# Expert stage of a two-layer diffusion backbone: loop over token tiles unrolled, weights made slot by slot on ScalarE

## The chip, the cores and the metric

The kernel runs on 1 core of one Trainium2 chip, which has a TensorE (PE, matmul), a VectorE (DVE), a ScalarE (ACT), a GpSimd (POOL) and a SyncE (SP), and 16 DMA engines. The metric is the device time of one execution in microseconds; less is better.

## The reference, cut to what matters

Two trunk layers work on 256 context and 512 latent tokens of width 1024. Each has a mixer and then an expert layer (PEER) with 8 heads; each head picks 16 of 16384 single-neuron experts for each token. Layer 0 runs the experts for all 768 tokens, layer 1 for the 512 latent ones.

```python
def peer_ffn(xn, wq, keys1, keys2, u_tab, v_tab):
    q = (xn @ wq).reshape(t, PEER_HEADS, PEER_D_KEY)
    s1 = jnp.einsum('thd,hkd->thk', q[..., :half], keys1)
    s2 = jnp.einsum('thd,hkd->thk', q[..., half:], keys2)
    v1, i1 = lax.top_k(s1, PEER_TOPK)
    v2, i2 = lax.top_k(s2, PEER_TOPK)
    cand = (v1[..., :, None] + v2[..., None, :]).reshape(t, PEER_HEADS, PEER_TOPK * PEER_TOPK)
    cs, ci = lax.top_k(cand, PEER_TOPK)
...
    expert = e1 * PEER_N_KEYS + e2
    gate = jax.nn.softmax(cs, axis=-1)
...
        ub = u_tab[eb]
        vb = v_tab[eb]
        act = jax.nn.gelu(jnp.einsum('td,thkd->thk', xb, ub), approximate=False)
        return jnp.einsum('thk,thkd->td', gb * act, vb)
```

The result is multiplied by a gate row and added to the stream h. All is float32.

## The kernel before, in words

`backbone` runs the modulation rows, mixer 0, the expert stage of layer 0 (6 tiles of 128 tokens), mixer 1, the expert stage of layer 1 (4 tiles) and a final norm. The change lies in `peer_stage` (L1128 to L1521) and the constants ahead of it.

A tile has TS = 128 slots: 8 heads of 16 chosen experts. For each slot POOL issues one indirect DMA (L1217) that gathers for each of the 128 tokens its own expert's row, 1024 numbers of u and 1024 of v, 8 KB for each partition and 1.05 MB in all, into one of RING = 8 ring buffers. Over both layers that is 10 tiles and 1280 gathers.

What is done with a slot, in order: VectorE multiplies the u half by the normalised tokens f and sums it (the dot, L1492, with an accumulator read). ScalarE makes Gelu of two dots at once (L1285). VectorE multiplies it by 1/sum and by the exponentials of the softmax (`coefficients`, L1459), for a pair of slots (PAIR = 2), and does so behind the first dot of the next pair. ScalarE scales the identity by each of the two coefficients (the diagonal, L1288). TensorE multiplies diagonal and v half, two 512-column matmuls per slot (L1372; the trace has four instructions for them), and adds up the 16 slots of a head in one of two PSUM pairs. The last matmul's semaphore `slot_free` lets POOL gather into this ring buffer again. Per head VectorE adds the PSUM pair to y (`head_sum`, L1467 and L1469), and at a tile's end multiplies y by the gate row and adds it to h (L1517, L1519). It waits for TensorE before both, and only then copies the next tile's f (L1485).

While the slots of a tile run, the next tile is prepared: the norm (ScalarE L1225 and L1228, VectorE L1391 to L1400 into fn), transposes, queries and scores on TensorE (L1307 to L1331) with copies on ScalarE, and **routing** on VectorE (`route`, L1402): for each head four pieces, top 16 of the first scores, top 16 of the second, top 16 of their 256 sums, and the table index. Its small instructions are chained by a semaphore (`link`, L1406). One piece is put behind each pair g (2 slots), four pairs for each head:

```python
ROUTE_NOW = {3: 6, 8: 7}
ROUTE_FIRST = {4 * n: LAG + n for n in range(NH - LAG)}
ROUTE_NEXT = {33 + 4 * n: n for n in range(NH - LAG)}
```

So heads 0 to 5 of the next tile are routed in slots 66 to 113, and heads 6 and 7 in the early slots of their own tile. In the first tile of a layer, heads 0 and 1 (LAG = 2) come before its first dot, and 2 to 7 in its slots 0 to 47. ScalarE makes Exp for one head at a time (`gate`, L1272), with a table load before it and one before the next Gelu.

Order of work: each engine has its own straight program, tied to the others by semaphores. The first and the last tile of each layer are written out; the tiles between (4 in layer 0, 2 in layer 1) are one loop body (`tiles`, L1190, `eng.Fori`) on each engine, and waits in it compare with a register. Waits inside a chain are followed by a semaphore increment of their own (`wait_apart`, L1180).

## Time and profile before

| what | value |
|---|---|
| median of 3 runs | 4596.92 us (4594.8 to 4597.45) |
| the profiled execution: span from first to last instruction | 4610.2 us |
| the profiled execution's own time | only its span is given |
| PE busy | 3609.0 us, 78% |
| DVE busy | 2865.6 us, 62% |
| ACT busy | 1156.5 us, 25% |
| POOL busy | 1501.2 us, 33% |
| gathers | 1280, 1342.26 MB, 72.4% of 16 engines' span |
| TensorE's mean granted clock | 0.921 |

How to read it: the span is one execution, taken by the hardware profiler, and it lies 13.3 us above the median of the runs. Busy times of the engines overlap. A busy PE is not a PE at its peak, since matmuls are pipelined. The granted clock is the share of TensorE's full clock. The rows further on name an engine, a source line, the operation, output and inputs by the program's names, shapes, how often, busy us and mean ns, and behind the bar the idle time ahead of it with what ended it.

### The profile page before, as it was taken

To read this page: it belongs to the slowest core of one execution; us is meant where nothing else is said; L and a number is where in the kernel's file an instruction comes from. 1 tells how busy PE (TensorE), PEld (TensorE's weight loads), DVE (VectorE), ACT (ScalarE), POOL (GpSimd) and SP (SyncE) were. 2 spreads that over 40 slices of the span, in tenths; PEclk is the share of its full clock that TensorE was granted. 3 is DMA by queue.
4 is the path that set the end of the run, shared out by engine and by line. 5 is a ranking of instruction groups with operands and counts; after the bars stand their busy time and mean duration, and the time that the engine had idled before them with its cause. 6 is when DMAs were issued, how large, how long until landed. Compare 5 with 4: busy or idle time off the path is not lost. (4 is left out here: it accounts for less than half of the span.)

```text
span 4610.2 us, 39123 instructions
## 1 busy us (share of the span) xinstructions
PE 3609.0 (78%) x10024; PEld 1742.9 (38%) x10024; DVE 2865.6 (62%) x7037; ACT 1156.5 (25%) x2826; POOL 1501.2 (33%) x1338
## 2 busy tenths in 40 slices
PE   8899968778768777777777778996877876877776
PEld 1288643323323323322322226784332332332222
DVE  2222358776766776676686555664877677677655
ACT  1121113222222222222222122561322222222212
POOL 0103114444434443443444331001443444344332
PEclk9998689999989999998999998998998999899899
DMA  8612059999999998998999982004999999899998
GB/s 297 245 64 73 10 205 369 388 373 392 398 358 366 409 373 361 398 378 341 415 375 394 421 370 92 1 1 170 372 392 377 374 400 383 357 406 383 381 421 342
DMA packets 233040, 1455.55 MB, mean 316 GB/s; under 512 B 25141, under 2 KB 25141, under 8 KB 67813
## 3 DMA queue, kind: packets, MB, share of 16 engines
q0 software_dynamic: 184320, 1342.26, 72.4%
q1 hardware_dynamic: 48392, 110.79, 6.7%
q8 instruction: 62, 1.02, 0.1%
q14 instruction: 170, 1.38, 0.1%
q10 hardware_dynamic: 96, 0.10, 0.0%
HBM read 1447.72 MB, written 5.34 MB: 315 GB/s over the span
## 5 line engine op out<-in xcount | busy, mean ns | idle before, releaser
L1372 PE MATMUL peer_py<-peer_ring,peer_diag 128*128 128x512 f32 x5120 | 2506.7, 639 | 874.8 <-ACT peer_diag L1288 874.5
L1217 POOL DMA_INDIRECT peer_ring<-in_uv_dram,peer_idx x1280 | 1416.6, 1107 | 2123.8 <-PE peer_py L1372 1848.4
L1492 DVE CUSTOM_DVE_ANT_0 peer_ring<-peer_ring,peer_f 128x1024 f32<-128x1024 f32 x1280 | 1565.6, 1226 | 769.4 <-DMA peer_ring<-in_uv_dram,peer_idx 722.8
L1372 PEld LDWEIGHTS peer_py<-peer_ring,peer_diag 128*128 128x128 f32 x5120 | 996.7, 202 | 2353.2 <-issue 1194.2
L1288 ACT ACTIVATE peer_diag<-ident,peer_coef 128x128 f32<-128x128 f32 x1280 | 444.1, 394 | 1880.1 <-DVE peer_coef L1459 1880.1
L1285 ACT ACTIVATE peer_gel<-peer_u 128x2 f32<-128x2 f32 x640 | 129.9, 203 | 733.8 <-DVE peer_u L1492 732.9
L318 DVE TENSOR_TENSOR m_w_low<-m_w_low_plain,m_w_high 128x2048 fp32r<-128x2048 f32 x26 | 61.0, 2347 | 218.1 <-ACT m_w_high L313 218.0
L326 PE MATMUL m_ps<-m_w_high,m_aT_high 128*128 128x512 f32 x416 | 164.8, 396 | 3.5 <-DVE m_v L750 1.8
L1208 POOL IOTA peer_iota<- 128x16 f32 x2 | 0.3, 144 | 503.8 <-POOLq L765 363.6
L326 PE MATMUL m_ps<-m_w_low,m_aT_high 128*128 128x512 f32 x416 | 162.6, 391 | 0.0
L1459 DVE SCALAR_TENSOR_TENSOR peer_coef<-peer_gel,peer_grec,peer_gexp 128x2 f32<-128x2 f32 x640 | 138.3, 216 | 10.0 <-ACT peer_gel L1285 9.9
L326 PE MATMUL m_ps<-m_w_high,m_aT_low 128*128 128x512 f32 x368 | 143.9, 391 | 0.0
L176 PE MATMUL mod_ps<-arena,silu 128*2 128x512 f32 x256 | 113.7, 603 | 17.9 <-DMA arena<-in_ada_w_dram 17.9
L1314 PE MATMUL peer_pb<-arena,peer_fT 128*128 128x512 f32 x256 | 120.3, 592 | 0.0
L1469 DVE TENSOR_TENSOR peer_y<-peer_y,peer_py 128x1024 f32<-128x1024 f32 x70 | 85.1, 1216 | 48.7 <-PE peer_py L1372 48.7
L1285 ACT ACT_TABLE_LOAD x84 | 107.8, 1283 | 1.5
L1492 DVE DVE_READ_ACCUMULATOR2_ANT peer_u<- 128x1 f32 x1280 | 104.7, 82 | 0.0
L313 ACT ACTIVATE m_w_high<-m_w_low_plain 128x2048 fp32r<-128x2048 f32 x26 | 49.8, 1913 | 209.5 <-DMA m_w_low_plain<-in_ev_w_in_dram 101.8
L1272 ACT ACT_TABLE_LOAD x78 | 100.1, 1283 | 1.4
L992 PE MATMUL m_ps<-m_aT_high_plain,m_aT_low_plain 128*128 128x128 f32 x576 | 84.2, 293 | 6.2 <-ACT m_aT_high_plain L889 5.8
L326 PEld LDWEIGHTS m_ps<-m_w_high,m_aT_high 128*128 128x128 f32 x416 | 78.7, 189 | 20.2 <-DVE m_v L750 2.0
L992 PEld LDWEIGHTS m_ps<-m_aT_high_plain,m_aT_low_plain 128*128 128x128 f32 x576 | 71.7, 197 | 35.0 <-ACT m_aT_low_plain L874 24.9
(198 smaller groups left out, 2915.7 us busy)
## 6 DMA issues: line engine op xcount, KB each, us to landing
arena<-in_ada_w_dram SPq DMA_DIRECT2D x16, 2048.0 KB, 8.9
peer_ring<-in_uv_dram,peer_idx POOLq DMA_INDIRECT x1280, 9.3
mod_rows_sb<-in_ada_w_dram SPq DMA_DIRECT2D x8, 2048.0 KB, 9.1
m_w_low_plain<-in_ev_w_in_dram SPq DMA_DIRECT2D x12, 1024.0 KB, 5.0
arena<-in_peer_wq_dram SPq DMA_DIRECT2D x2, 4096.0 KB, 18.4
mod_rows_sb<-mod_rows SPq DMA_DIRECT2D x7, 1024.0 KB, 7.0
m_w_low_plain<-in_od_w_in_dram SPq DMA_DIRECT2D x6, 1024.0 KB, 5.2
m_w_low_plain<-in_ev_w_out_dram SPq DMA_DIRECT2D x4, 1024.0 KB, 5.0
```

The lines of the kernel that those rows point to most:

```text
L176: ins = pe.matmul(ps[:, n % 4], silu[:, :, k], ada[n % ring][:, k], start=k == 0, stop=k == KC - 1)
L326: ins = pe.matmul(out, l, r, start=j % 2 == 0 and kl == 0 and m == 0, stop=j % 2 == 1 and kl == KH - 1 and m == 2)
L992: ins = pe.matmul(PS[:, 4 + m // 4, (m % 4) * P:(m % 4 + 1) * P], pr[:, i % 3, m * P:(m + 1) * P], dg[:, i % 2], start=True, stop=True, sk ...
L1217: pool.indirect_dma_start(ring[:, s % RING], None, A["uv"], bass.IndirectOffsetOnAxis(idx[:, hd, j:j + 1], 0)).then_inc(sem(f"landed{s % R ...
L1272: act.activation(gexp[:, hd], cs[:, hd], ACT.Exp, bias=negm[:, hd:hd + 1], accum_out=gsum[:, hd:hd + 1]).then_inc(sem("gexp"), 1)
L1285: act.activation(gel[:, g % 4], u[:, g % 4], ACT.Gelu).then_inc(sem("gelu"), 1)
L1288: act.activation(diag[:, (PAIR * g + j) % RING], ident[:], ACT.Copy, scale=coef[:, g % 4, j:j + 1]).then_inc(sem("diag"), 1)
L1314: ins = pe.matmul(PB[:, 2 + b], fT[:, k], wq[:, k, b * HALF:(b + 1) * HALF], start=k == 0, stop=k == KC - 1)
L1372: ins = pe.matmul(PY[:, hd % 2, b], diag[:, s % RING], ring[:, s % RING, D + b * HALF:D + (b + 1) * HALF], start=s % TOPK == 0, stop=s % T ...
L1459: dve.scalar_tensor_tensor(coef[:, g % 4], gel[:, g % 4], grec[:, hd:hd + 1], gexp[:, hd, at:at + PAIR], ALU.mult, ALU.mult).then_inc(sem( ...
L1469: dve.tensor_tensor(y[:], y[:], ps, ALU.add).then_inc(sem("y_free"), 1)
L1492: dve.tensor_tensor_reduce(x, x, f[:], 1.0, 0.0, ALU.mult, ALU.add, u[:, g % 4, j:j + 1]).then_inc(sem("dot"), 1)
```

## The change

- The tile loop is gone: every engine's program is written out for all tiles, and all waits compare with constants. POOL's waits and the links lose the extra semaphore increment.
- Slot by slot (`weight`): ScalarE makes Gelu of one slot, multiplies it by the normalised gate (a Copy with a scale per partition) and makes the diagonal, each with a wait on its own step before. VectorE's `coefficients` is gone.
- `combine`: all 128 slots of a tile are summed in one PSUM pair, which alternates from tile to tile. `head_sum` is gone; `add_up` multiplies the PSUM pair by the gate row and adds it to h, behind dot 4 of the next tile.
- f, cs, idx and the gates are double-buffered; fn and its copy are gone.
- The softmax: VectorE subtracts the top score for a batch of heads, ScalarE makes one Exp for the batch, and VectorE sums, inverts and multiplies (`normalise`). Batches are 4 heads; in a layer's first tile 2, 3 and 3.
- Routing: in the first tile of a layer the own heads 2 to 7 as before, one piece every second slot in slots 0 to 47. The next tile's 32 pieces are spread evenly from slot 45 (first tile: 52) to slot 120.
- Queries, their transposes and scores are made in two halves.

```diff
@@
+TS = NH * TOPK
+PIECES = 4
+ACT_SQUARE, DVE_MEAN, ACT_ROOT, DVE_MOD = 1, 3, 5, 8
+PE_F_T, ACT_F_T, PE_Q = 11, 14, 16
+ACT_Q, PE_Q_T, ACT_Q_T, PE_S, ACT_S = (25, 33), (27, 35), (29, 37), (31, 39), (34, 42)
+FIRST_GATES, GATES = ((0, 2), (2, 5), (5, 8)), ((0, 4), (4, 8))
+def own_piece(s):
+    return (LAG + s // 2 // PIECES, s // 2 % PIECES) if s % 2 == 0 and 0 <= s // 2 < (NH - LAG) * PIECES else None
+def next_piece(s, start, n=NH * PIECES):
+    span = TS - 5 - start
+    for m in range(n):
+        if start + m * span // n == s:
+            return divmod(m, PIECES)
+    return None
@@ POOL
+            for i in range(first, last + 1):
+                for s in range(TS):
+                    n, (hd, k) = i * TS + s, divmod(s, TOPK)
+                    if k == 0:
+                        pool.wait_ge(sem("idx"), i * NH + hd + 1)
+                    if n >= RING:
+                        pool.wait_ge(sem("slot_free"), n - RING + 1)
+                    pool.indirect_dma_start(ring[:, n % RING], None, A["uv"], bass.IndirectOffsetOnAxis(idx[:, i % 2, hd, k:k + 1], 0)
+                                            ).then_inc(sem(f"landed{n % RING}"), 16)
@@ ScalarE
-                    act.wait_ge(sem("dot"), i * TS + PAIR * (g + 1))
-                    act.activation(gel[:, g % 4], u[:, g % 4], ACT.Gelu).then_inc(sem("gelu"), 1)
-                    act.wait_ge(sem("coef"), i * PAIRS_T + g + 1)
-                    for j in range(PAIR):
-                        act.activation(diag[:, (PAIR * g + j) % RING], ident[:], ACT.Copy, scale=coef[:, g % 4, j:j + 1]
-                                       ).then_inc(sem("diag"), 1)
+            def exponents(i, b):
+                lo, hi = gates_of(i)[b]
+                act.wait_ge(sem("shifted"), batch_ready(i, lo))
+                act.activation(gexp[:, lo:hi], shifted[:, lo:hi], ACT.Exp).then_inc(sem("gexp"), 1)
+            def weight(i, s):
+                n, (hd, k) = i * TS + s, divmod(s, TOPK)
+                at = slice(n % RING, n % RING + 1)
+                act.wait_ge(sem("dot"), n + 1)
+                act.activation(gel[:, at], u[:, at], ACT.Gelu).then_inc(sem("gelu"), 1)
+                if k == 0:
+                    act.wait_ge(sem("gate"), batch_ready(i, hd))
+                act.wait_ge(sem("gelu"), n + 1)
+                act.activation(coef[:, at], gel[:, at], ACT.Copy, scale=gate[:, i % 2, hd, k:k + 1]).then_inc(sem("coef"), 1)
+                act.wait_ge(sem("coef"), n + 1)
+                act.activation(diag[:, n % RING], ident[:], ACT.Copy, scale=coef[:, at]).then_inc(sem("diag"), 1)
@@ TensorE
+            def combine(i, s):
+                n = i * TS + s
+                if s == 0 and i >= 2:
+                    pe.wait_ge(sem("y"), i - 1)
+                pe.wait_ge(sem("diag"), n + 1)
+                for b in range(2):
+                    ins = pe.matmul(PY[:, i % 2, b], diag[:, n % RING], ring[:, n % RING, D + b * HALF:D + (b + 1) * HALF],
+                                    start=s == 0, stop=s == TS - 1)
+                ins.then_inc(sem("slot_free"), 1)
@@ VectorE
-                dve.scalar_tensor_tensor(coef[:, g % 4], gel[:, g % 4], grec[:, hd:hd + 1], gexp[:, hd, at:at + PAIR],
-                                         ALU.mult, ALU.mult).then_inc(sem("coef"), 1)
+            def below_top(i, b):
+                lo, hi = gates_of(i)[b]
+                c = cs[:, i % 2, lo:hi]
+                dve.tensor_tensor(shifted[:, lo:hi], c, c[:, :, 0:1].broadcast_to([P, hi - lo, TOPK]), ALU.subtract
+                                  ).then_inc(sem("shifted"), 1)
+            def normalise(i, b):
+                lo, hi = gates_of(i)[b]
+                dve.wait_ge(sem("gexp"), batch_ready(i, lo))
+                link(dve.tensor_reduce(gsum[:, lo:hi], gexp[:, lo:hi], AX.X, ALU.add))
+                link(dve.reciprocal(grec[:, lo:hi], gsum[:, lo:hi]))
+                dve.tensor_tensor(gate[:, i % 2, lo:hi], gexp[:, lo:hi],
+                                  grec[:, lo:hi].rearrange("p (h o) -> p h o", o=1).broadcast_to([P, hi - lo, TOPK]), ALU.mult
+                                  ).then_inc(sem("gate"), 1)
+            def add_up(i):
+                dve.wait_ge(sem("slot_free"), (i + 1) * TS)
+                if i == first:
+                    dve.wait_ge(S("peer_gates"), 16 * rows_loads)
+                dve.tensor_tensor(y[:], PY[:, i % 2].rearrange("p b n -> p (b n)"), rows[:, kind(i - shift), 2], ALU.mult).then_inc(sem("y"), 1)
+                dve.wait_ge(sem("y"), i + 1)
+                link(dve.tensor_tensor(h[:, i - shift], h[:, i - shift], y[:], ALU.add))
...
+            dve.wait_ge(sem("idx"), first * NH + LAG)
+            below_top(first, 0)
+            normalise(first, 0)
+            for i in range(first, last + 1):
+                for s in range(TS):
+                    dot(i, s)
+                    if i > first and s == 4:
+                        add_up(i - 1)
+                    if i < last:
+                        if s == DVE_MEAN:
+                            mean(i + 1)
+                        if s == DVE_MOD:
+                            modulate(i + 1)
+                    for tile, piece, past in ((i, own_at(i, s), own_at(i, s - 3)), (i + 1, next_at(i, s), next_at(i, s - 3))):
+                        if piece is not None:
+                            route(tile, *piece)
+                        if batch_ending(tile, piece) is not None:
+                            below_top(tile, batch_ending(tile, piece))
+                        if batch_ending(tile, past) is not None:
+                            normalise(tile, batch_ending(tile, past))
+            add_up(last)
```

## Rows read from the trace of the kernel before

**Rows 1.** Page, part 2: mean busy share of the DMA engines, 40 slices of the span

```profile
DMA  8612059999999998998999982004999999899998
```

**Rows 2.** Table by stretch: length, busy us per engine, clock, DMA share, GB/s

```profile
1225.00:1330.00 105.00, 78.78 (x153) 30.62 (x154) 90.97 (x263) 30.18 (x75) 47.06 (x38) 0.92 0.97 377
...
1465.00:1565.00 100.00, 86.41 (x223) 36.87 (x221) 58.55 (x125) 20.63 (x61) 41.56 (x41) 0.98 1.01 420
```

**Rows 3.** Waits, 1225 to 1330 us: sum, times, longest in us

```profile
DVE peer_ring L1492 <- DVE peer_topi L1418: 1.5, 8, 0.2
```

**Rows 4.** Waits, 1465 to 1565 us

```profile
DVE peer_ring L1492 <- DMA peer_ring<-in_uv_dram,peer_idx: 38.9, 32, 2.3
```

**Rows 5.** From issue of a gather to landing, 1225 to 1330, then 1465 to 1565 us

```profile
DMA to landing us min/median/max: 6.4/8.2/10.6
...
DMA to landing us min/median/max: 7.5/9.9/11.0
```

**Rows 6.** Timeline, end of layer 0: two dots ten slots apart, one group of matmuls

```profile
2706.17 1.23 DVE L1492 CUSTOM_DVE_ANT_0 peer_ring<-peer_ring,peer_f 128x1024 f32<-128x1024 f32 x1 [1.11 <-DMA peer_ring<-in_uv_dram,peer_idx]
...
2710.51 3.70 PE L1372 MATMUL peer_py<-peer_ring,peer_diag 128*128 128x512 f32 x8 [1.27 <-ACT peer_diag L1288]
...
2731.00 1.23 DVE L1492 CUSTOM_DVE_ANT_0 peer_ring<-peer_ring,peer_f 128x1024 f32<-128x1024 f32 x1 [1.11 <-DMA peer_ring<-in_uv_dram,peer_idx]
```

**Rows 7.** Timeline of VectorE while routing: start us, us, engine, line, operation

```profile
1302.71 1.23 DVE L1492 CUSTOM_DVE_ANT_0 peer_ring<-peer_ring,peer_f 128x1024 f32<-128x1024 f32 x1
...
1304.00 1.22 DVE L1492 CUSTOM_DVE_ANT_0 peer_ring<-peer_ring,peer_f 128x1024 f32<-128x1024 f32 x1
...
1307.33 1.29 DVE L1492 CUSTOM_DVE_ANT_0 peer_ring<-peer_ring,peer_f 128x1024 f32<-128x1024 f32 x1 [0.19 <-DVE peer_topi L1418]
...
1312.01 1.29 DVE L1492 CUSTOM_DVE_ANT_0 peer_ring<-peer_ring,peer_f 128x1024 f32<-128x1024 f32 x1 [0.19 <-DVE peer_topi L1418]
...
1318.17 1.23 DVE L1492 CUSTOM_DVE_ANT_0 peer_ring<-peer_ring,peer_f 128x1024 f32<-128x1024 f32 x1
...
1324.38 1.23 DVE L1492 CUSTOM_DVE_ANT_0 peer_ring<-peer_ring,peer_f 128x1024 f32<-128x1024 f32 x1
```

**Rows 8.** Page, part 5: head sums

```profile
L1469 DVE TENSOR_TENSOR peer_y<-peer_y,peer_py 128x1024 f32<-128x1024 f32 x70 | 85.1, 1216 | 48.7 <-PE peer_py L1372 48.7
```

**Rows 9.** Timeline of VectorE at a seam between tiles (1345 to 1432 us)

```profile
1372.32 0.69 DVE L1485 COPY peer_f<-peer_fn 128x1024 f32<-128x1024 f32 x1 [5.62 <-issue]
1377.61 1.23 DVE L1492 CUSTOM_DVE_ANT_0 peer_ring<-peer_ring,peer_f 128x1024 f32<-128x1024 f32 x1 [4.59 <-issue]
...
1378.76 1.22 DVE L1492 CUSTOM_DVE_ANT_0 peer_ring<-peer_ring,peer_f 128x1024 f32<-128x1024 f32 x1
```

**Rows 10.** First and last dot of all, last dot of layer 0, first of layer 1

```profile
L1492 DVE CUSTOM_DVE_ANT_0 peer_ring<-peer_ring,peer_f x1280: 1204/1225/1297, 661.5 to 4585.1; 128x1024 f32<-128x1024 f32 x183
...
2750.88 1.23 DVE L1492 CUSTOM_DVE_ANT_0 peer_ring<-peer_ring,peer_f 128x1024 f32<-128x1024 f32 x1 [1.06 <-DMA peer_ring<-in_uv_dram,peer_idx]
...
3206.58 1.23 DVE L1492 CUSTOM_DVE_ANT_0 peer_ring<-peer_ring,peer_f 128x1024 f32<-128x1024 f32 x1
```

**Rows 11.** Page, part 5, and Exp in the groups of 1200 to 1550 us

```profile
L1288 ACT ACTIVATE peer_diag<-ident,peer_coef 128x128 f32<-128x128 f32 x1280 | 444.1, 394 | 1880.1 <-DVE peer_coef L1459 1880.1
L1285 ACT ACTIVATE peer_gel<-peer_u 128x2 f32<-128x2 f32 x640 | 129.9, 203 | 733.8 <-DVE peer_u L1492 732.9
...
L1285 ACT ACT_TABLE_LOAD x84 | 107.8, 1283 | 1.5
...
L1272 ACT ACTIVATE peer_gexp<-peer_cs,peer_negm 128x16 f32<-128x16 f32 x8 | 2.5, 308 | 0.1
```

**Rows 12.** Timeline of the first tile: dots of slots 16 and 32

```profile
708.44 1.23 DVE L1492 CUSTOM_DVE_ANT_0 peer_ring<-peer_ring,peer_f 128x1024 f32<-128x1024 f32 x1
...
752.99 1.23 DVE L1492 CUSTOM_DVE_ANT_0 peer_ring<-peer_ring,peer_f 128x1024 f32<-128x1024 f32 x1
```

**Rows 13.** Timeline of TensorE after a longer pause

```profile
1320.02 5.38 PE L1372 MATMUL peer_py<-peer_ring,peer_diag 128*128 128x512 f32 x8 [2.39 <-ACT peer_diag L1288]
```

More of the change, by code:

```diff
@@ L1363, in body @@
-            def body(i, now, nxt):
-                for g in range(PAIRS_T):
-                    hd = g // PAIRS
-                    if g % PAIRS == 0:
-                        pe.wait_ge(sem("y_free"), i * NH + hd + 1)
-                    for j in range(PAIR):
-                        s = PAIR * g + j
-                        pe.wait_ge(sem("diag"), i * TS + s + 1)
-                        for b in range(2):
-                            ins = pe.matmul(PY[:, hd % 2, b], diag[:, s % RING], ring[:, s % RING, D + b * HALF:D + (b + 1) * HALF],
-                                            start=s % TOPK == 0, stop=s % TOPK == TOPK - 1)
-                        ins.then_inc(sem("slot_free"), 1)
-                    if not nxt:
+                    queries(first, part, k)
@@ L1376, in body @@
+                q_transposes(first, part)
+                scores(first, part)
+            for i in range(first, last + 1):
+                for s in range(TS):
+                    combine(i, s)
+                    if i == last:
                         continue
-                    if g == PE_F_T:
+                    if s == PE_F_T:
                         f_transposes(i + 1)
-                    if PE_Q <= g < PE_Q + KC:
-                        queries(i + 1, g - PE_Q)
-                    if g == PE_Q_T:
-                        q_transposes(i + 1)
@@ L1383, in body @@
-                    if PE_S <= g < PE_S + 2:
-                        scores(i + 1, g - PE_S)
-            tiles(pe, body)
+                    if PE_Q <= s < PE_Q + 2 * KC:
+                        queries(i + 1, (s - PE_Q) // KC, (s - PE_Q) % KC)
+                    for part in range(2):
+                        if s == PE_Q_T[part]:
+                            q_transposes(i + 1, part)
+                        if s == PE_S[part]:
+                            scores(i + 1, part)
         @block.vector
@@ L1402, in route @@
[L1402 to L1423 removed]
+                link(dve.reciprocal(ss[:, 3:4], ss[:, 2:3]))
@@ L1424, in route @@
+            def route(i, hd, piece):
+                if piece == 0 and hd % 4 == 0:
+                    dve.wait_ge(sem("s"), 2 * i + hd // 4 + 1)
                 if piece < 2:
@@ L1521, in _ @@
-            tiles(dve, body)
+            dve.wait_ge(sem("idx"), first * NH + LAG)
+            below_top(first, 0)
+            normalise(first, 0)
+            for i in range(first, last + 1):
+                for s in range(TS):
+                    dot(i, s)
+                    if i > first and s == 4:
+                        add_up(i - 1)
+                    if i < last:
+                        if s == DVE_MEAN:
[9 more added lines that the diff above has]
+                            normalise(tile, batch_ending(tile, past))
```

332 lines of the change are left out of this document (110 added, 222 removed).

## The prediction

> **What bounds the kernel now.** I first read the page's slices by time [rows 1]: outside the first fifth and the short mixer stage in the middle, the 16 DMA engines are busy in nine tenths of nearly every slice, so the two expert stages look bound by the gathers. The table by stretch [rows 2] shows that this is two cases. From 1465 to 1565 us the gathers move 420 GB/s and VectorE is busy for 58.55 of 100 us. From 1225 to 1330 us, where VectorE also routes the next tile, they move 377 GB/s at a share of 0.97, and VectorE is busy for 90.97 of 105 us. The waits settle who leads. In the routing stretch VectorE's dot product never waited for a landing: the longest wait before it is 1.5 us in sum, for its own routing [rows 3]. In the other it waited 32 times, 38.9 us, for a landing [rows 4]. The time from issue to landing agrees: median 8.2 us while routing, 9.9 us else [rows 5], so at 2.7 and 2.5 us per slot some 3.0 and 4.0 gathers are in flight. A busy share near 1 is no sign of a full queue here: fewer are in flight, and each packet is open longer.
>
> So there are two paces. **DMA's pace:** ten slots of the last tile of layer 0 take 2731.00 - 2706.17 = 24.83 us, 2.483 us per slot [rows 6]. **Routing pace:** four pairs with the four pieces of one head take 1324.38 - 1302.71 = 21.67 us, 2.71 us per slot [rows 7], and a head sum of 1.22 us [rows 8] comes on top every 16 slots. A third loss is the seam between tiles: VectorE drains TensorE (48.7 us of waiting before head sums, 10 times [rows 8]) and then stands 5.62 and 4.59 us at "issue" around a loop's end [rows 9]. From the first to the last dot, layer 0 takes 2750.88 - 661.5 = 2089.4 us for 767 intervals and layer 1 4585.1 - 3206.58 = 1378.5 us for 511 [rows 10]: 3467.9 us, 2.713 per slot. At DMA's pace these 1278 intervals would take 3173 us; some 295 us are the most that the expert stages can give.
>
> **The change part by part.**
>
> VectorE, per pair of slots: two dots and a coefficient take 1304.00 - 1302.71 = 1.29 plus 1.15, 2.44 us; back to back dots without one are 1378.76 - 1377.61 = 1.15 us apart [rows 7, 9], so 2.30 us stay. The pieces cost 4.62, 4.68, 6.16 and 6.21 less 2.44 each: 2.18, 2.24, 3.72 and 3.77, 11.9 us per head. They stay, less two one-column instructions (a negation, a reciprocal), which I put at 0.1 us each. Per tile the change adds one subtraction, one sum, one reciprocal and one product for each batch of heads, some 1 us per batch of small instructions (estimate from the 0.1 to 0.3 us steps inside the pieces); it comes twice per tile and is in the jitter below.
>
> Spread over 78 slots, one head's pieces fall on 9.75 slots: 11.9 + 9.75 x 1.15 = 23.1 us, 2.37 us per slot, under 2.483. VectorE stops being the bound there, but is filled to 95%. In the first tile of each layer the own heads 2 to 7 still fall on 8 slots each: (11.7 + 9.2) / 8 = 2.62 us for 48 slots; its next-tile pieces fall on 8.9 slots, (11.9 + 10.2) / 8.9 = 2.49, level with DMA.
>
> ScalarE: per slot a Gelu (0.203), a coefficient and a diagonal (0.394) [rows 11]. The coefficient has no row: at least the Gelu's 0.203, at most the 0.308 of an Exp of 16 columns with a per-partition operand [rows 11]; I take 0.3. With two waits on itself, 0.05 to 0.3 us each (the trace has none of this kind), a slot takes 1.0 to 1.5 us of 2.483: it hides behind the gathers. Were that cover gone, ScalarE would set 1.5 us, still below the dot's pace with pieces. Exp in batches leaves 22 in place of 80, so most table loads of 1.28 us [rows 11] go; they were hidden, and I count nothing. A late batch would hold the next Gelu for about 3 us, and behind it diagonal, matmul, slot and gather; the ring covers that.
>
> The ring: before, a pair's coefficient is made only after the next pair's first dot, so the first slot of a pair waits from 1302.71 to past 1307.33 + 1.2 = 1308.5 [rows 7] before its diagonal is begun. After, the diagonal is ready 1.0 to 1.5 us behind the dot. Slots come free about 5 us earlier, two gathers more in flight. That is what lets the DMA queue stay full over a piece of 3.7 us.
>
> TensorE: the same matmuls into one PSUM pair, 3.70 us per two slots [rows 6], 1.85 of 2.483. The seven other head sums per tile vanish and the tile's last is folded into the gate product, off the seam: VectorE does it behind dot 4 of the next tile while eight slots are in the ring. The seam's drain and the loop's end go. What would be late next there is nothing but the landing of the next slot.
>
> POOL issues the same 1280 gathers; waits on constants replace register waits; it is queued behind nothing new. idx and cs are doubled, so the next tile's indices, spread to slot 120, are there before POOL wants them. SP has the same loads.
>
> **The sum.** Layer 0: 48 x 2.62 + 719 x 2.483 = 125.8 + 1785.3 = 1911.1; layer 1: 125.8 + 463 x 2.483 = 1275.4. Together 3186.5, a gain of 281.4 us. Less:
> - routing stretches at 2.533 rather than 2.483. The bounds are 2.483 and 2.71 [rows 6, 7]; I take a value near the lower, because VectorE no longer leads by its rows, and add 0.05 for jitter: 78 slots x 8 tiles x 0.05 = 31 us;
> - mean and modulation of the next tile, 3 us of VectorE in the part of each first tile where it leads: 6 us;
> - before the first dot, the first Exp batch now ends behind both heads' routing and VectorE waits for it: 1.28 + 0.31 us [rows 11] and three small steps, 2.5 us per layer: 5 us;
> - back: at each stage's end one head sum (1.22) and one slot's matmuls (1.85) are no longer in the tail: 6 us.
>
> 281.4 - 31 - 6 - 5 + 6 = 245 us. Against the profiled span of 4610.2 us that is 4365; that execution lies 13.3 us above the median of the runs, 4596.9, and the same saving there gives **4352 us**.
>
> The Trainium skill, "DMA: Bandwidth & Descriptors", Anatomy of one DMA, fits bytes / 436e3 us behind a fixed part; for 1.05 MB that is 2.405 us per slot, an estimate that would put the sum near 4352 - 1230 x 0.078 = 4256 us. The trace does not agree: 2.483 us is held over ten slots.
>
> **The rivals.**
>
> Gathers are the bound in routing stretches as well. For it: their share is 0.97 there, and 377 / 0.97 = 389 GB/s would be 2.70 us per slot whatever VectorE does [rows 2]. Against it: no dot waits for a landing [rows 3]. Then 624 slots take 2.70: 135 us in place of 31, 4456 us. A ring that runs dry behind each long piece ends between the two. Chance 0.20.
>
> Straight code starves an engine's instruction fetch, which the loop bodies did not. For it: the 5.62 and 4.59 us at "issue" [rows 9] show what a missing fetch costs. Against it: the first tile is straight code already, and its second head takes 752.99 - 708.44 = 44.55 us [rows 12], as 2 x 21.67 + 1.22 = 44.6 in a loop body. With one such pair of stalls per tile, 10 x 10.2 = 102 us: 4454 us. Chance 0.08.
>
> On the other side: **TensorE's clock.** Eight matmuls that follow 2.39 us of idle time took 5.38 rather than 3.70 us [rows 13]: part of them ran at the lower of the two levels, 1.2 in place of 2.4 GHz. Now TensorE gets one slot at a time, with a pause after each, and behind a piece of 3.7 us it stands for about 3 us. At the lower level throughout a slot takes some 3.5 us, more than 2.483, and TensorE leads: each such slot adds 1.0 us that the ring cannot give back. From 245 / 1.02 = 240 such slots on, 38% of the 624, the change is slower than before; if all 624 are, 4352 - 31 + 624 x 1.02 = 4957 us. Against it: in the DMA-bound stretch, with pauses of 1.27 us between pairs [rows 6], the granted clock is 0.98 [rows 2], and per-slot pauses are shorter (2.483 - 1.85 = 0.63). A backlog also fills the pause behind a piece. Chance 0.06, of which 0.05 slower.
>
> The Trainium skill, "TensorE: Matmul & The Clock Gate", HAM oscillation, describes this rival: a kernel whose matmul groups are short beside the waits between them is throttled again at each wait. By that rule the routing stretches would fall to it; the trace agrees only in so far as a pause of over 2 us was followed by slow matmuls.
>
> **How the numbers follow.** The forecast has 0.66, with its own range of 4310 to 4400 (no jitter at all; half of the way to 2.70). The two rivals near 4455 have 0.28, the clock 0.06. The range of 4305 to 4460 leaves out the clock rival and some of what lies beyond the others. About 0.2% is what a measurement of this kernel can tell from no change: faster 0.94, same 0.01, slower 0.05.
>
> **What the new profile would show.** Right: dots 2.48 to 2.55 us apart over whole tiles, also in slots 45 to 123; DMA near 415 GB/s in every full slice; dots that wait for landings in the routing stretches; no gap at the seam beyond a slot's; median issue to landing over 11 us; ScalarE busy about 1 us per slot. The forecast is wrong if the routing stretches keep 2.7 us per slot with waits for landings (first rival), if "issue" ends many waits (second), or if the granted clock falls under 0.8 and gathers wait for TensorE (third).

## The result and the profile after

The changed kernel takes 4339.51 us (median of 4 runs, 4336.71 to 4348.3) against 4597.18 us before (median of 4, 4594.8 to 4603.24): a ratio of 0.9437, 95% interval 0.9423 to 0.945. That is 257.7 us less, where 245 were forecast. The profiled execution has a span of 4334.8 us and a time of its own of 4336.71 us.

From the page of the changed kernel: the slices by time (PEclk is the granted TensorE clock in tenths), the groups of the expert stages, and the issue of the gathers with its median time to landing.

```profile
span 4334.8 us, 33292 instructions
PEclk9899599999999999999999999998999999999999
DMA  8712029999999999999999982003999999999998
L1445 DVE CUSTOM_DVE_ANT_0 peer_ring<-peer_ring,peer_f 128x1024 f32<-128x1024 f32 x1280 | 1556.1, 1224 | 918.6 <-DMA peer_ring<-in_uv_dram,peer_idx 909.9
L1228 POOL DMA_INDIRECT peer_ring<-in_uv_dram,peer_idx x1280 | 1451.7, 1134 | 1817.9 <-PE peer_py L1345 1692.5
L1275 ACT ACTIVATE peer_diag<-ident,peer_coef 128x128 f32<-128x128 f32 x1280 | 513.8, 401 | 41.7
L1273 ACT ACTIVATE peer_coef<-peer_gel,peer_gate 128x1 f32<-128x1 f32 x1280 | 377.1, 295 | 46.7 <-ACT peer_gel L1269 0.4
peer_ring<-in_uv_dram,peer_idx POOLq DMA_INDIRECT x1280, 14.9
```

The DMA slices look much as in [rows 1], only with fewer 8s, so the busy share again says little. What has changed is who waits. The dots wait for landings for 909.9 us in sum, and that nearly everywhere but in the first 48 slots of each layer. The next two fences are the second tile, which routes the third: the table by stretch (length, busy us of PE, PEld, DVE, ACT, POOL, clock, DMA share, GB/s), for that tile and for the last tile of layer 0, which routes nothing; then the waits of the second tile (sum, times, longest).

```profile
980.00:1300.00 320.00, 262.26 (x588) 102.81 (x587) 228.14 (x540) 127.66 (x399) 147.58 (x128) 0.97 1.01 420
2270.00:2580.00 310.00, 245.72 (x496) 84.09 (x496) 155.27 (x250) 111.40 (x373) 120.20 (x120) 1.00 1.00 416
```

```profile
POOL peer_ring L1228 <- PE peer_py L1345: 166.1, 118, 4.1
DVE peer_ring L1445 <- DMA peer_ring<-in_uv_dram,peer_idx: 86.5, 79, 2.1
```

Where the routing stretch moved 377 GB/s before [rows 2], a whole routing tile now moves 420, as much as the one without routing (its stretch from 1145 to 1265 us, about slots 68 to 116, moves 419). Of its 128 dots 79 wait for a landing, where before no such wait was seen [rows 3]. VectorE no longer leads.

The seam between the first and the second tile, timeline: the last two dots of the old tile, the first of the new.

```profile
970.03 1.22 DVE L1445 CUSTOM_DVE_ANT_0 peer_ring<-peer_ring,peer_f 128x1024 f32<-128x1024 f32 x1 [1.25 <-DMA peer_ring<-in_uv_dram,peer_idx]
...
972.51 1.23 DVE L1445 CUSTOM_DVE_ANT_0 peer_ring<-peer_ring,peer_f 128x1024 f32<-128x1024 f32 x1 [1.25 <-DMA peer_ring<-in_uv_dram,peer_idx]
...
975.00 1.23 DVE L1445 CUSTOM_DVE_ANT_0 peer_ring<-peer_ring,peer_f 128x1024 f32<-128x1024 f32 x1 [1.25 <-DMA peer_ring<-in_uv_dram,peer_idx]
```

It is a slot like any other, 2.49 us, where the drain and the loop's end [rows 9] made gaps of 11.4 to 21.8 us. Worked out from the starts of the dots in both traces, us per 16 slots (at 2.483 per slot: 39.7):

```
slots           0-15  -31   -47   -63   -79   -95   -111  -127+seam   tile
before, tile 0  47.0  44.5  44.3  38.1  46.7  44.5  44.3  49.3       358.7
before, tile 1  40.0  42.7  41.5  39.8  45.0  44.5  44.5  59.4       357.5
after,  tile 0  39.8  37.8  40.1  43.3  40.9  40.1  41.5  38.1       321.5
after,  tile 1  40.7  39.7  40.1  40.6  41.9  38.1  41.2  40.2       322.7
after,  tile 6  39.8  37.7  39.8  45.0  39.4  40.3  41.4  38.9       322.1
```

From the first to the last dot, layer 0 now takes 2582.7 - 653.5 = 1929.2 us and layer 1 4313.3 - 3028.3 = 1285.0 us: 3214.2 us, or 2.515 per slot for 1278 intervals, against 3467.9 before [rows 10]. The other 21.7 us of the spans' difference (275.4) lie outside: the first dot comes 8.0 us earlier, the way from the last dot of layer 0 to the first of layer 1 is 10.1 us shorter (445.6 for 455.7), and the tail 3.6.

Part of the early start is one thing that the diff does and the prediction never priced. Routing of head 0 ahead of the first dot, VectorE's timeline. Before (first instruction, one link inside, first of the next head):

```profile
637.11 0.29 DVE L1414 MAX8 peer_top<-peer_scores 128x8 f32<-128x128 f32 x1 [16.99 <-ACT peer_scores L1266]
...
638.31 0.29 DVE L1417 MAX8 peer_top<-peer_scores 128x8 f32<-128x128 f32 x1
...
638.75 0.09 DVE L1418 MATCH_VALUE_LOAD peer_topi<-peer_top,peer_scores 128x8 f32 x1
...
648.86 0.29 DVE L1414 MAX8 peer_top<-peer_scores 128x8 f32<-128x128 f32 x1 [0.17 <-DVE peer_idx L1445]
```

After:

```profile
633.62 0.29 DVE L1396 MAX8 peer_top<-peer_scores 128x8 f32<-128x128 f32 x1 [17.11 <-ACT peer_scores L1257]
...
634.66 0.29 DVE L1399 MAX8 peer_top<-peer_scores 128x8 f32<-128x128 f32 x1
...
634.99 0.09 DVE L1400 MATCH_VALUE_LOAD peer_topi<-peer_top,peer_scores 128x8 f32 x1
...
642.98 0.28 DVE L1396 MAX8 peer_top<-peer_scores 128x8 f32<-128x128 f32 x1
```

The durations are the same, the steps between are not: from one instruction to the one that needs its result it took 0.44 us, now 0.33; one head took 11.75 us and takes 9.36. In the kernel before every such wait is followed by a semaphore increment on VectorE; the change leaves it out. Experiment 3 gives that 2.07 us of a head's 2.39.

The other surprise is in the first tile of each layer. Timeline of the first tile, slots 46 to 51:

```profile
769.45 0.17 DVE L1424 TENSOR_SCALAR peer_idx<-peer_ef 128x16 uint32<-128x16 f32 x1
...
769.72 1.02 ACT L1257 ACTIVATE peer_scores<-peer_pb 128x1024 f32<-128x1024 f32 x1 [12.23 <-DVE peer_idx L1424]
...
771.65 7.75 PE L1345 MATMUL peer_py<-peer_ring,peer_diag 128*128 128x512 f32 x14 [11.25 <-ACT peer_diag L1275]
...
775.38 0.94 POOL L1228 DMA_INDIRECT peer_ring<-in_uv_dram,peer_idx  x1 [13.13 <-PE peer_py L1345]
```

ScalarE's second copy of the next tile's scores, put behind slot 42, overwrites scores that own head 7 is still routed from; that ends at slot 46. So ScalarE stands 12.23 us with the weights of several slots queued behind the copy, TensorE and then POOL stand with it (POOL issues nothing for 13.13 us), and the dots of slots 51 and 52 wait 2.43 and 2.18 us for their landings, twice the usual 1.25. These are the 43.3 and 45.0 in the table.

### The profile page after: what moved, and what is told of

Same layout as the page of the kernel before. It is cut to its first block and busy times, and to the rows that moved or that the text cites. A ratio compares the mean times of both kernels' runs of the same rounds, so it can differ in the third digit from the quotient of the medians.

```text
span 4334.8 us, 33292 instructions
## 1 busy us (share of the span) xinstructions
PE 3589.7 (83%) x10024; PEld 1674.6 (39%) x10024; DVE 2684.7 (62%) x6235; ACT 1564.1 (36%) x4522; POOL 1536.3 (35%) x1338
## 5 line engine op out<-in xcount | busy, mean ns | idle before, releaser
L1445 DVE CUSTOM_DVE_ANT_0 peer_ring<-peer_ring,peer_f 128x1024 f32<-128x1024 f32 x1280 | 1556.1, 1224 | 918.6 <-DMA peer_ring<-in_uv_dram,peer_idx 909.9
L1228 POOL DMA_INDIRECT peer_ring<-in_uv_dram,peer_idx x1280 | 1451.7, 1134 | 1817.9 <-PE peer_py L1345 1692.5
L1345 PEld LDWEIGHTS peer_py<-peer_ring,peer_diag 128*128 128x128 f32 x5120 | 929.3, 194 | 2148.7 <-ACT peer_diag L1275 1320.4
L1269 ACT ACTIVATE peer_gel<-peer_u 128x1 f32<-128x1 f32 x1280 | 258.8, 202 | 1827.0 <-DVE peer_u L1445 1825.7
L1275 ACT ACTIVATE peer_diag<-ident,peer_coef 128x128 f32<-128x128 f32 x1280 | 513.8, 401 | 41.7
L1273 ACT ACTIVATE peer_coef<-peer_gel,peer_gate 128x1 f32<-128x1 f32 x1280 | 377.1, 295 | 46.7 <-ACT peer_gel L1269 0.4
L1320 PE MATMUL peer_pb<-arena,peer_fT 128*128 128x512 f32 x320 | 164.6, 612 | 2.4 <-ACT peer_fT L1242 2.4
L1320 PEld LDWEIGHTS peer_pb<-arena,peer_fT 128*128 128x128 f32 x320 | 62.5, 197 | 81.3 <-issue 81.1
L990 PE MATMUL m_ps<-m_aT_high_plain,m_aT_low_plain 128*128 128x128 f32 x576 | 84.5, 294 | 7.2 <-ACT m_aT_high_plain L887 5.8
L254 POOL TENSOR_TENSOR m_a<-m_a,mod_rows_sb 128x1024 f32<-128x1024 f32 x6 | 15.1, 2518 | 202.9 <-DVE m_a L238 202.9
L324 PEld LDWEIGHTS m_ps<-m_w_low,m_aT_high 128*128 128x128 f32 x416 | 78.9, 190 | 16.8
## 6 DMA issues: line engine op xcount, KB each, us to landing
peer_ring<-in_uv_dram,peer_idx POOLq DMA_INDIRECT x1280, 14.9
```

Of the source, the lines that this page charges most:

```text
L324: ins = pe.matmul(out, l, r, start=j % 2 == 0 and kl == 0 and m == 0, stop=j % 2 == 1 and kl == KH - 1 and m == 2)
L990: ins = pe.matmul(PS[:, 4 + m // 4, (m % 4) * P:(m % 4 + 1) * P], pr[:, i % 3, m * P:(m + 1) * P], dg[:, i % 2], start=True, stop=True, sk ...
L1228: pool.indirect_dma_start(ring[:, n % RING], None, A["uv"], bass.IndirectOffsetOnAxis(idx[:, i % 2, hd, k:k + 1], 0)).then_inc(sem(f"lande ...
L1269: act.activation(gel[:, at], u[:, at], ACT.Gelu).then_inc(sem("gelu"), 1)
L1273: act.activation(coef[:, at], gel[:, at], ACT.Copy, scale=gate[:, i % 2, hd, k:k + 1]).then_inc(sem("coef"), 1)
L1275: act.activation(diag[:, n % RING], ident[:], ACT.Copy, scale=coef[:, at]).then_inc(sem("diag"), 1)
```

## The experiments

Questions: how the gain divides between the loop's end, the increments, the spread of the routing, the early weights and the seam; and what the 41 us are that the stages still lie above 1278 x 2.483 = 3173. Two kernels start from the old one, the others from the new.

**1. Old kernel, loop written out.**

```diff
-            body(first, ROUTE_FIRST, ROUTE_NEXT)
-            with eng.Fori(first + 1, first + n_tiles - 1) as i:
-                body(i, ROUTE_NOW, ROUTE_NEXT)
-            body(first + n_tiles - 1, ROUTE_NOW, {})
+            last = first + n_tiles - 1
+            for i in range(first, last + 1):
+                body(i, ROUTE_FIRST if i == first else ROUTE_NOW, ROUTE_NEXT if i < last else {})
```

> The kernel before with its tile loop written out, nothing else. Theory (a loop's end costs at the seam): the four seams behind a loop's end are some 10.5 us longer per tile in the trace of before (355 to 357 us against 345 to 347 us), so 4597 - 42 = 4555 us. Rival (the loop's end is hidden by the ring, the long seams have another cause): 4597 us.

Measured 4553.86 us (before on the same chip 4603.97), 0.9893 [0.9877, 0.991]: 50 us, where 42 were expected. The seam of tile 0 in its timeline:

```profile
1000.66 1.23 DVE L1491 CUSTOM_DVE_ANT_0 peer_ring<-peer_ring,peer_f 128x1024 f32<-128x1024 f32 x1 [1.11 <-DMA peer_ring<-in_uv_dram,peer_idx]
...
1007.28 1.22 DVE L1468 TENSOR_TENSOR peer_y<-peer_y,peer_py 128x1024 f32<-128x1024 f32 x1 [4.90 <-PE peer_py L1371]
...
1011.78 1.23 DVE L1491 CUSTOM_DVE_ANT_0 peer_ring<-peer_ring,peer_f 128x1024 f32<-128x1024 f32 x1
```

The waits for "issue" are gone and the gap is the same 11.1 us, 1011.78 - 1000.66, at nearly every seam: the drain, the head sum, the gate product, the sum into h and the copy of f. So no engine stands for want of straight code, and writing the loop out was worth 50 us: its end, and with it the waits that compared with a register, which this run does not tell apart. Routing slots still take 44 to 45 us per 16.

**2. The same, and no increment behind a wait,** neither in VectorE's chains nor on POOL.

```diff
         def wait_apart(eng, which, value):
...
-            eng.sem_inc(sem("passed_" + ("pool" if eng is nc.gpsimd else "dve")), 1)
```

> The same, and without the semaphore increment of its own behind each wait of a routing chain and of POOL. Theory (each of the 19 increments of a head costs VectorE about 0.12 us, and VectorE leads in the routing stretches): a head's four pieces fall from 11.9 to some 9.7 us, 30 groups of 16 slots fall from 44.5 to 40.5 us, with the starts some 150 us: 4405 us. Rival (the gain of the change comes from ScalarE's coefficients, the spread and the earlier free slots, the increments cost nothing beside the chain's own latency): 4555 us.

Measured 4409.25 us (4395.29 to 4412.78), 0.9564 [0.9546, 0.9582]: another 145 us, the largest single part. With coefficients still on VectorE, pairs, head sums and old places of the pieces, the routing groups of 16 slots fall from 44 to 45 us to between 40.3 and 43.7 us. Waits from 1170 to 1300 us in this kernel:

```profile
ACT peer_diag L1286 <- DVE peer_coef L1457: 77.9, 26, 5.2
DVE peer_ring L1490 <- DMA peer_ring<-in_uv_dram,peer_idx: 12.4, 13, 2.1
```

Dots now wait for landings while VectorE routes. What is left to the new kernel's 4339.5 is 70 us. By spans (4411.0 and 4334.8) they lie 46.6 us in layer 0 (1975.8 for 1929.2), 19.6 in layer 1 (1304.6 for 1285.0) and 10 outside. More than half of those in the layers lie at the seams: the 16 slots ahead of a seam and the 16 behind it take 84.5 us on average here, gap included, and 79.7 in the new kernel, 38 us over eight seams.

**3. New kernel, increment put back behind each link.**

```diff
                 dve.wait_ge(sem(f"link{layer}"), links)
+                dve.sem_inc(sem("passed_dve"), 1)
```

> The changed kernel with the increment put back behind each wait of VectorE's chains. Theory (increments cost 0.12 us each, and the spread keeps VectorE below the gathers' pace all the same): pieces back at 11.9 us; only the first tiles and the starts lose, 12 + 9 + some jitter: 4365 us. Rival (the increments alone gave the gain): some 4480 us.

Measured 4381.87 us, 0.9516 [0.95, 0.9532]: 42 us more than the new kernel (36 by the two ratios, as the chips differ), 17 more than expected. The spread tiles hardly feel it: 322.9, 323.2, 325.0, 323.3 us, for 322.7, 322.1, 323.4, 322.1, some 6 us over all of both layers. The rest is in the two first tiles (335.4 and 335.6, for 321.5 and 322.1; their groups are 44.5, 42.4, 41.5, 45.0), 27 us, and outside the stages (1131.8 us for 1120.6). Slots 0 to 47 take 128.4 us. My terms gave 48 x 2.62 + 3 = 128.8 for them: the arithmetic was right, for a kernel that keeps its increments. From 660 to 780 us no dot waits for a landing:

```profile
POOL peer_ring L1228 <- PE peer_py L1345: 68.7, 39, 8.9
ACT peer_gel L1269 <- DVE peer_u L1446: 61.5, 35, 5.4
...
DVE peer_ring L1446 <- DVE peer_topi L1401: 2.2, 12, 0.2
```

**4. The same, and the pieces as dense as before.** One piece every two slots from slot 62, all 32 of them.

```diff
-    span = TS - 5 - start
-    for m in range(n):
-        if start + m * span // n == s:
-            return divmod(m, PIECES)
+    m = (s - 62) // 2
+    if s % 2 == 0 and 0 <= m < n:
+        return divmod(m, PIECES)
```

> The changed kernel with the increments back and the next tile's pieces one every two slots from slot 62. Theory (VectorE leads again at 2.62 us per slot for 64 slots in 8 tiles): 4365 + 60 = 4425 us. Rival (earlier free slots carry it whatever VectorE does): 4365 us.

Measured 4386.64 us, 0.9526 [0.951, 0.9542]: 5 us over the one before; the rival was right. Groups 4 to 6 of the middle tiles (counted from 0) are slower, 41.4 to 42.9, but the next tile's first is 36.2 to 38.5 instead of 39.8: VectorE falls behind while routing, ready slots pile up in the ring, and the next tile works them off. The spreading that I took for the core of the change is worth about 5 us, increments in, once weights are made at once and no seam drains the ring.

**5. Weights begun late again.** On top of 4, the first slot of a pair waits for the next pair's first dot, as the old coefficient did.

```diff
-                act.wait_ge(sem("dot"), n + 1)
+                act.wait_ge(sem("dot"), n + (3 if s < TS - 2 and s % 2 == 0 else 2 - s % 2))
```

> As a_link_inc_dense, and ScalarE begins a pair's weights only behind the next pair's first dot, as the kernel before did: the slots come free late. Theory (the ring can carry VectorE's lag over a dense routing stretch only because slots come free early): with about two fewer gathers in flight the 64 slots at 2.62 us per tile are no longer carried, 4387 + 8 x 9 = 4460 us. Rival (the ring carries the lag either way, the freeing time is worth nothing): 4387 us.

Measured 4420.16 us, 0.9603 [0.9587, 0.9619]: 33.5 us over kernel 4. Tiles of layer 0 take 326.4 to 329.0 us for 323.1 to 324.9, the seam is 4.4 us, and first tiles 341.8 and 342.8. So freeing slots early matters where VectorE is near its limit (this kernel has the increments and the dense pieces; without them it was not tried), with about half of the price that I had expected.

**6. Second scores copy six slots later in first tiles.**

```diff
-                            if s == ACT_S[part]:
+                            if s == (ACT_S[part] + 6 if part and i == first else ACT_S[part]):
```

> The changed kernel with the second half of the scores copied 6 slots later in each layer's first tile, behind the own head 7's indices. Theory (ScalarE's wait of 12.2 us for those indices holds Gelu, diagonals and slots and leaves two gaps of some 2.4 us between landings per layer): 4339.5 - 9.5 = 4330 us. Rival (the gaps come from the gathers themselves): 4339.5 us.

Measured 4334.78 us (4330.9 to 4336.23; before there 4603.23), 0.9413 [0.9397, 0.9429]. First tiles take 319.7 and 319.2 us, the group 3 of each 40.1 and 40.4. In its timeline the copy starts without a wait:

```profile
778.99 0.40 ACT L1275 ACTIVATE peer_diag<-ident,peer_coef 128x128 f32<-128x128 f32 x1
779.30 1.01 ACT L1257 ACTIVATE peer_scores<-peer_pb 128x1024 f32<-128x1024 f32 x1
```

The stall is shown and cost some 5 us in all, half of the 9.5 that I had expected: 7.8 us in the two groups, of which the later ones give back a part (the two tiles are 4.7 us shorter). By medians it is 5 to 6 us under the new kernel (4339.51, and 4340.93 in the control below); the intervals overlap, the tile times don't.

**7. The drain put back on the seam.** The last tile's sum ahead of the next tile's first dot.

```diff
                 for s in range(TS):
+                    if i > first and s == 0:
+                        add_up(i - 1)
                     dot(i, s)
-                    if i > first and s == 4:
-                        add_up(i - 1)
```

> The changed kernel with a tile's sum taken ahead of the next tile's first dot: VectorE drains TensorE at each of the 8 seams, but no loop ends there. Theory (some 7 us of VectorE per seam are covered by the gathers in the ring): 4340 to 4350 us. Rival (the drain itself cost the kernel before): 4339.5 + 8 x 7 = 4395 us.

Measured 4341.17 us, 0.9429 [0.9413, 0.9444]: no difference. The gap at a seam is 6.8 us, and the next 16 slots take 35 to 37. With eight slots in the ring, made free one by one, the drain is covered. In the kernel of experiment 2 it was not, 84.5 us for 79.7 over the same 32 slots (79.9 here). That slots freed late, the last pair's coefficient and the copy of f made the difference is likely, but no run takes them apart.

**8. Coefficient back on VectorE, slot by slot** (from kernel 6; a product of 128 x 1 behind the next dot).

```diff
@@ ScalarE
-                if k == 0:
-                    act.wait_ge(sem("gate"), batch_ready(i, hd))
-                act.wait_ge(sem("gelu"), n + 1)
-                act.activation(coef[:, at], gel[:, at], ACT.Copy, scale=gate[:, i % 2, hd, k:k + 1]).then_inc(sem("coef"), 1)
@@ VectorE
+            def coefficient(n):
...
+                dve.wait_ge(sem("gelu"), n + 1)
+                if k == 0:
+                    dve.wait_ge(sem("gate"), batch_ready(i, hd))
+                dve.tensor_tensor(coef[:, at], gel[:, at], gate[:, i % 2, hd, k:k + 1], ALU.mult).then_inc(sem("coef"), 1)
```

> As a_scores_later, and the coefficient is made on VectorE, slot by slot, behind the next slot's dot. Theory (a slot comes free 2.5 us later, VectorE has 0.15 us more per slot; the ring covers both): 4330 to 4345 us. Rival (ScalarE's coefficient is what keeps the slots free in time): over 4370 us.

Measured 4349.48 us, 0.9448 [0.9433, 0.9464]: 15 us over kernel 6, just above what was expected. The first tiles are 2.4 and 2.7 us longer, the others up to 1.4. Which part of the 15 is the later diagonal, and which VectorE's load, this run does not tell; the 1.0 us in each of the two tiles without routing has its explanation in the last section.

**9. Ring of 9** (from kernel 6) and **10. ring of 6** (from the new kernel).

```diff
-RING = 8
+RING = 9
```

> As a_scores_later, with 9 ring buffers in place of 8. Theory (what is left over the gathers' own pace, some 40 us, is half jitter that a further gather in flight takes up, half a 0.96 us step every 64 slots that it does not): 4335 - 10 = 4325 us. Rival (all of the rest is in the gathers): 4335 us.

```diff
-RING = 8
+RING = 6
```

> The changed kernel with 6 ring buffers. Theory (8 buffers hold two more gathers than the steady pace of 2.483 us needs, and the two carry the pieces of routing): the stretches without routing stay at 39.8 us per 16 slots, those with it rise to some 42: 4339 + 40 = 4380 us, less than the kernel before. Rival (the gathers need their four or five in flight for the pace itself): every group of 16 slots rises, over 4450 us.

Measured 4335.46 us, 0.9425 [0.9412, 0.9438], no gain over kernel 6 where 10 us were expected; and 4367.66 us, 0.9497 [0.948, 0.9513], 27 us over the control where 40 were. The gathers' rows on the two pages, ring of 9 and ring of 6:

```profile
peer_ring<-in_uv_dram,peer_idx POOLq DMA_INDIRECT x1280, 17.4
```

```profile
peer_ring<-in_uv_dram,peer_idx POOLq DMA_INDIRECT x1280, 10.0
```

At 2.5 us per slot that is 7.0 and 4.0 gathers in flight, 6.0 with a ring of 8. The pace of the plain tiles is the same in all three (317.5 us from the first to the last dot of tile 5, 317.4 with 8). Four in flight are enough, then. The ring of 6 loses in its first tiles (335.1 and 335.2 us; group 3, with the 12 us stall, is 49.2 and 50.6), not in all routing stretches as its theory had it, and 1 to 2 us in some others. With the stall gone a ninth buffer gives nothing that the median shows: what is left is not a lack of gathers in flight.

**11. Exp, sum and gate for one head at a time.**

```diff
-FIRST_GATES, GATES = ((0, 2), (2, 5), (5, 8)), ((0, 4), (4, 8))
+FIRST_GATES = GATES = tuple((hd, hd + 1) for hd in range(NH))
```

> The changed kernel with batches of one head: 80 Exp instead of 22, each with its two table loads, and 8 instead of 2 normalisations per tile on VectorE. Theory (both lie beside the gathers): 4340 to 4348 us. Rival (a table load that holds the next Gelu by 2.9 us, eight times per tile, holds slots): over 4360 us.

Measured 4352.11 us (4344.51 to 4357.83), 0.9464 [0.9448, 0.948]: 11 us over the control, between the two theories. By spans it is 7.9 us: 2.9 and 2.1 in the first tiles, 1.2 ahead of the first dot and 1.1 between the layers; the middle tiles keep their 321.9 to 323.4 us. The batches are hidden where the ring has slack, and worth a little where it has not.

**12. Control: the new kernel once more.**

> The changed kernel once more, as the measure for the three beside it on the same chip: 4339 us, 0.944 of the kernel before.

Measured 4340.93 us, 0.9439 [0.9425, 0.9453]: as at first.

## Why the prediction was right, and where not

The forecast was 4352 us in a range of 4305 to 4460, the result 4339.5. The mechanism holds in the order in which it was put:

- **Two paces, one of them VectorE's.** Right. In the routing stretches of before no dot waited for a landing [rows 3], now 79 do in one tile, and GB/s rose from 377 to 420. The rival that the gathers are the bound there too (2.70 us per slot, 43.2 us per 16 slots) is refuted by groups of 38.1 to 42.3 us. The pace itself held over the whole last tile of layer 0: 2582.7 - 2265.3 = 317.4 us for 127 intervals, 2.50. The 2.405 us that the Trainium skill's fit gives ("DMA: Bandwidth & Descriptors", Anatomy of one DMA) was reached in no tile. (The forecast's 4256 us for it counts 1230 slots where its sum has 1182 at that pace; that moves it by 4 us.)
- **Straight code.** The rival with long "issue" waits is refuted: seams of 2.5 us, and experiment 1 gains 50 us with the code written out. The packets that bring the instructions do seem to cost the gathers something, with or without a loop (last section).
- **TensorE's clock.** Granted 0.97 in the routing tile (0.94 from 1145 to 1265 us, where the routing is densest) and 0.953 over the span (0.921 before): the upper level nearly throughout, in spite of one pause per slot. The Trainium skill, "TensorE: Matmul & The Clock Gate", HAM oscillation, would have matmul groups that are short beside the waits between them throttled again at each wait; in this kernel that did not come about. Its matmuls are not short beside the waits either: 245.72 us for 496 instructions, four per slot, is 1.98 us, and the pause behind them about 0.5.
- **ScalarE.** Gelu, coefficient and diagonal are 0.20, 0.295 and 0.40 us, and their waits on each other some 0.03 to 0.09. The slot of 978.75 us ends at 979.31 + 0.40: 0.96 us, just under the 1.0 to 1.5 of the forecast.

Three of its rows show the chain of one slot (timeline of ScalarE in the changed kernel):

```profile
978.75 0.20 ACT L1269 ACTIVATE peer_gel<-peer_u 128x1 f32<-128x1 f32 x1 [1.46 <-DVE peer_u L1445]
...
978.99 0.29 ACT L1273 ACTIVATE peer_coef<-peer_gel,peer_gate 128x1 f32<-128x1 f32 x1
...
979.31 0.40 ACT L1275 ACTIVATE peer_diag<-ident,peer_coef 128x128 f32<-128x128 f32 x1
```

- **Slots free about 5 us earlier, two gathers more in flight.** Right in size: issue to landing is 14.9 us for 8.2 to 9.9 [rows 5], at 2.5 us per slot 6.0 gathers for 3.0 and 4.0. That this is what keeps the queue full is true only where VectorE is near its limit (experiment 5); in the kernel as it is, the ring of 6 keeps the pace with four in flight.
- **Seam.** Right that nothing but the next landing is late there. Wrong in why it matters: put back, the drain costs nothing (experiment 7).

What failed is a step of the part on VectorE: "The pieces cost 4.62, 4.68, 6.16 and 6.21 less 2.44 each ... They stay". They did not. The diff takes one semaphore increment out of every link, and I gave that no term. A head costs 9.4 us in place of 11.75 (2.07 of it the increments, by experiment 3), and four sums follow from it:

- The first tiles' 48 slots at 2.62 us (125.8 us per layer, and 3 for mean and modulation) took 117.7 and 117.3 us. VectorE is nearly full there but holds no gather back: it starts some 4 us behind the landings and works that off, busy for 79.0 of the 82 us from 653 to 735 us without a dot that waits for a landing, while the gathers move 421 GB/s. Mis-sized by 11 us per layer. With the increments in, the first 48 slots take 128.4 us, as forecast, and the gathers move only 388 GB/s (660 to 780 us).
- Two heads stand ahead of the first dot of each layer: the stages start earlier. The forecast had them 2.5 us later, for the Exp batch. That batch took from 652.45 to the gate's start at 653.35 us, about 1 us, since the load of Exp's table was done before. Outside the stages the forecast was some 20 us too high; experiment 3 gives 11.2 of them to the increments, the rest is mostly the Exp and a start of routing that came 3.5 us earlier (first dots of kernels with the same opening vary from 653.4 to 657.9 us). Before, the copy of f stood in the place of the Exp batch: from the last index to the first dot it took 661.47 - 660.41 = 1.06 us, now 653.46 - 652.24 = 1.22.
- VectorE is not "filled to 95%" while routing: 9.4 / 9.75 + 1.15 = 2.11 of 2.483 us, 85%.
- The price of the increments is 145 us in the old kernel (POOL's among them) and some 40 in the new one (VectorE's alone). In the old one VectorE led wherever it routed, in the new one, with them put back, only in its first tiles.

The jitter term (31 us) has about the right size for other reasons. Outside the 2 x 48 first slots 1182 intervals took 2979 us, 44 over 2.483 each. Some 9 of that is ScalarE's stall (3.5 and 5.2 us in the two groups), which the forecast did not see: it asked what is queued behind a late Exp, not behind a copy that needs a buffer back. Some 32 is a step of 0.96 us that comes 33 times in these slots (last section), which the forecast did not have; little is left for jitter.

One more step helped by chance. I took the saving from a profiled execution 13.3 us above the median and subtracted it from the median. But the new kernel's stages were built up from rates, and such a sum forecasts the new span itself, 4365 us, to which an excess of the old execution adds nothing. The span came out at 4334.8, 30 us off (9 in the stages, 21 outside); the median only 12.5. Where in the old execution its 13.3 us lay, no row tells.

**The gain in order:** loop written out 50, increments 145, all the rest 70 us (4604.0, 4553.9, 4409.3, 4339.5, the last on another chip whose kernel before was 6.8 us faster). These shares hold in this order. The rest cannot be divided by undoing single parts, because each part covers for the others: the drain is worth 0, the spread 5, the coefficient up to 15, the Exp batches 11, early weights 33 where VectorE is loaded. The lowest median is that of experiment 6, at 0.9413; a ring of 9 on top of it, 0.9425, is the same within the intervals.

## What to carry to other kernels

A transfer engine that is busy 9 slices in 10 may still wait for the compute engine that frees its buffers: look in each stretch for which wait ends last, and for the time from issue to landing. In a chain of small dependent instructions, count what stands between them: a semaphore increment of its own behind each wait cost 145 us in the old kernel, nearly three times what writing out the loop gave. A ring of buffers pays for late work on any engine if its slots come free one by one as soon as they can; then it hardly matters where that work is put, and single long waits (a buffer wanted back too early) are the next thing to look for.

## What the runs showed of the hardware

- An increment behind a wait on VectorE costs 0.11 us per link (0.44 for 0.33 us from start to start), 2.07 us for a head with 19 links (11.43 for 9.36 us, the new kernel with and without). The Trainium skill, "VectorE: DVE Perf Modes", The DRAIN you can't avoid, says that a semaphore on each instruction costs nothing extra in a chain. If that is the increment which the instruction itself carries, both kernels here have it and no run tests it. The one priced here is an instruction by itself.
- A step of 0.96 us. In the last tile of layer 0, where nothing is routed, dots are 2.48 us apart, but the dot of slot 23 comes 3.46 us after the one before, and so again 64 slots on. Three dots of that tile in the timeline:

```profile
2319.96 1.22 DVE L1445 CUSTOM_DVE_ANT_0 peer_ring<-peer_ring,peer_f 128x1024 f32<-128x1024 f32 x1 [1.25 <-DMA peer_ring<-in_uv_dram,peer_idx]
...
2323.42 1.23 DVE L1445 CUSTOM_DVE_ANT_0 peer_ring<-peer_ring,peer_f 128x1024 f32<-128x1024 f32 x1 [2.22 <-DMA peer_ring<-in_uv_dram,peer_idx]
...
2325.91 1.22 DVE L1445 CUSTOM_DVE_ANT_0 peer_ring<-peer_ring,peer_f 128x1024 f32<-128x1024 f32 x1 [1.26 <-DMA peer_ring<-in_uv_dram,peer_idx]
```

  It looks like a step every 64 gathers, but it goes with VectorE's instructions. In the routing tiles, where VectorE has more to do per slot, landings 3.4 to 3.5 us apart come every 19 to 27 gathers (slots 54, 77, 99 and 122 of the second tile). In the kernel of experiment 8, where VectorE has one product more in each slot, they come at slots 7, 44 and 86 of the tile without routing, three in place of two, and that tile is 1.0 us longer. Between two steps lie 128 of VectorE's recorded instructions in the tile without routing and 107 to 141 in the others. With the ring of 9, 33 of the 37 steps come at the same gather. And a packet of the instruction queue q14 goes out 1.5 to 3.6 us ahead of the late landing: so for 35 of the 37 such landings in the new kernel and for 38 of 38 with the ring of 9, where it would be 7 of 100 by chance. From the DMA view of the new kernel from 2320 to 2322 us, then two dots of experiment 8, slots 43 and 44:

```profile
q14 instruction: 1, 0.01, 1.1%
```

```profile
2380.39 1.23 DVE L1441 CUSTOM_DVE_ANT_0 peer_ring<-peer_ring,peer_f 128x1024 f32<-128x1024 f32 x1 [1.18 <-DMA peer_ring<-in_uv_dram,peer_idx]
...
2383.86 1.22 DVE L1441 CUSTOM_DVE_ANT_0 peer_ring<-peer_ring,peer_f 128x1024 f32<-128x1024 f32 x1 [2.16 <-DMA peer_ring<-in_uv_dram,peer_idx]
```

  35 x 0.96 = 34 us in all, of the 41 that the stages lie above 3173. That the packet which brings VectorE its next instructions delays the gather is the reading that fits all of this; no run was made for it, and why one packet of 8 KB costs 0.96 us stays open. It is no price of straight code alone: the kernel with the loop has 170 packets on q14, the one of experiment 1 has 117, the new one 101, and that of experiment 3, with some 1500 increments more on VectorE, 112.
- In the tiles without routing the pace of the gathers did not depend on how many were in flight, from 4.0 to 7.0. More in flight only made each longer, 10.0, 14.9 and 17.4 us.
